# The router of a mixture-of-experts layer: order of its VectorE work, register loads, split gather and the start of the expert products

## What is computed

```python
aff = sigmoid(xt @ router_w)                       # 256 tokens, 16 experts in 4 groups of 4
biased = aff + router_bias
group_score = sum(top_k(biased grouped by 4, 2))   # best two of each group
g_sel = argmax(group_score)                        # one group for each token
e_idx = top_k(where(in_group, biased, -inf), 2)    # two experts inside it
gates = one_hot(e_idx) * aff / sum of the two
out = sum_e (silu(xt @ w_gate[e]) * (xt @ w_up[e]) * gates[e]) @ w_down[e]   # 1024 -> 512 -> 1024
```

## Time and profile before

| | |
|---|---|
| median of 3 runs | 3359.07 us (3356.76 to 3362.08) |
| the profiled execution | 3353.76 us, its span 3351.9 us |
| mean granted TensorE clock | 0.96 of full speed |
| busy | PE 92%, PEld 72%, DVE 49%, ACT 31% of the span |
| instructions | 40558 |
| HBM | 475.95 MB read, 142 GB/s over the span |

### The profile page before, as it was taken

The page is one execution under the profiler, slowest core; times in us unless marked ns, Lnnn a source line. Parts: engine busy times, 40 slices in busy tenths (PEclk is TensorE's granted clock), DMA queues, the critical chain, the costliest instruction groups (busy, mean ns, idle before and its releaser), DMA issues.

```text
span 3351.9 us, 40558 instructions
## 1 busy us (share of the span) xinstructions
PE 3070.9 (92%) x16552; PEld 2410.8 (72%) x16552; DVE 1642.7 (49%) x2593; ACT 1047.7 (31%) x1584; POOL 16.4 (0%) x56
## 2 busy tenths in 40 slices
PE   8779999988999799998997877899999999986998
PEld 7568876766887588884445777378886888855898
DVE  1545487245448643333975666263335324324554
ACT  2333376234337622222022111142224222132333
POOL 0000000000000000000000000000000000000000
PEclk9999999989999899999998888999999999998999
DMA  6437698544779722223122000322221222220452
GB/s 257 181 132 287 264 354 311 179 167 174 278 271 349 284 85 92 100 100 127 69 80 91 1 1 1 151 92 96 101 100 63 100 101 91 85 76 0 148 179 101
DMA packets 69102, 479.22 MB, mean 143 GB/s; under 512 B 7376, under 2 KB 10832, under 8 KB 11728
## 3 DMA queue, kind: packets, MB, share of 16 engines
q1 hardware_dynamic: 67616, 473.16, 37.8%
q10 hardware_dynamic: 1328, 3.87, 0.3%
HBM read 475.95 MB, written 1.05 MB: 142 GB/s over the span
## 4 chain that ended last, share of the span: by engine, by line
PE 68%; PEld 8%; DVE 8%; issue 6%; ACT 4%; PEldq 3%; DMA 2%; DVEq 0%; ACTq 0%; SPq 0%
PE ps L541 18%; PE ps L542 18%; PE ps L543 18%; PEld ps L533 8%; PE ps L533 2%; PE ps L1473 1%; PE ps L1764 1%; PE ps L2075 1%; DMA ring<-in_ada 1%; PE ps L1488 1%; PE ps L2087 1%; ACT w_hi L554 1%; PE ps L2346 1%; PE ps L808 1%; PE ps L1545 1%
## 5 line engine op out<-in xcount | busy, mean ns | idle before, releaser
L562 DVE TENSOR_TENSOR w_lo<-ring,w_hi 128x1024 fp32r<-128x1024 f32 x552 | 671.1, 1224 | 712.1 <-ACT w_hi L554 705.7
L554 ACT ACTIVATE w_hi<-ring 128x1024 fp32r<-128x1024 f32 x552 | 582.2, 1058 | 922.5 <-PE ps L543 767.3
L541 PE MATMUL ps<-x_hi,w_hi 128*128 128x512 f32 (+1 forms) x1408 | 514.8, 366 | 23.2 <-DVE x_lo L928 12.5
L542 PE MATMUL ps<-x_lo,w_hi 128*128 128x512 f32 (+1 forms) x1408 | 513.3, 365 | 0.0
L543 PE MATMUL ps<-x_hi,w_lo 128*128 128x512 f32 (+1 forms) x1408 | 513.2, 364 | 0.0
L541 PEld LDWEIGHTS ps<-x_hi,w_hi 128*128 128x128 f32 x1408 | 268.1, 190 | 68.9 <-issue 24.1
L533 PE MATMUL ps<-HM,ring 128*128 128x256 f32 (+1 forms) x928 | 296.6, 481 | 12.4 <-DVEq L963 3.7
L542 PEld LDWEIGHTS ps<-x_lo,w_hi 128*128 128x128 f32 x1408 | 268.1, 190 | 41.4
L543 PEld LDWEIGHTS ps<-x_hi,w_lo 128*128 128x128 f32 x1408 | 267.8, 190 | 41.7
L533 PEld LDWEIGHTS ps<-HM,ring 128*128 128x128 f32 x928 | 177.5, 192 | 129.1 <-issue 110.4
L541 PE MATMUL ps<-h_hi,w_hi 128*128 128x512 f32 (+1 forms) x704 | 255.2, 362 | 0.0
(11 more groups left out here) (407 smaller groups left out, 4448.8 us busy)
## 6 DMA issues: line engine op xcount, KB each, us to landing
ring<-in_moe_up SPq DMA_DIRECT2D x128, 1024.0 KB, 5.2
ring<-in_ff_up SPq DMA_DIRECT2D x88, 1024.0 KB, 4.7
ring<-in_ada SPq DMA_DIRECT2D x72, 1024.0 KB, 6.2
ring<-in_moe_down SPq DMA_DIRECT2D x64, 1024.0 KB, 5.2
ring<-in_ff_down SPq DMA_DIRECT2D x44, 1024.0 KB, 4.7
ring<-in_w_in SPq DMA_DIRECT2D x14, 1024.0 KB, 7.6
ring<-in_even_in SPq DMA_DIRECT2D x10, 1024.0 KB, 4.7
ring<-in_w_o SPq DMA_DIRECT2D x8, 1024.0 KB, 7.5
```

The lines of the kernel that those rows point to most:

```text
L541: pe.matmul(dst, hi, xh, start=start, stop=False, skip_group_check=True)
L542: pe.matmul(dst, hi, xl, start=False, stop=False, skip_group_check=True)
L554: act.activation(w_hi[:, j % HALVES, :], ring[:, u % SLOTS, (j % 2) * D:(j % 2 + 1) * D], ACT.Copy)\
L562: dve.tensor_tensor(w_lo[:, j % HALVES, :], ring[:, u % SLOTS, (j % 2) * D:(j % 2 + 1) * D], w_hi[:, j % HALVES, :].bitcast(F32), ALU.subt ...
```

## The change

- DVE: the eight m_lo move from the head of `router_dve` to behind S_; the routing starts at once. Behind them the low halves 0 and 1 of the first unit are made, ahead of the gates; halves 2 and 3 stay behind the gates.
- SP: only the first group id is read before the first expert transfer; the three others are read before the first unit of another rank, the fifth.
- Gather: the turned x is kept as a high part XT_hi (ACT's copy, now to fp32r) and a low part XT_lo (DVE, `turned_rest(0)` ahead of the wait for "counts", `turned_rest(1)` behind S_). S_ is now written as fp32r, S_r. The two products of each k become four, all with fp32r operands. Groups 6 and 7 go to banks 2 and 3 and wait for ACT's copies 2 and 3; all groups wait for `turned_rest(1)`.
- PE: `moe_pe` no longer waits for the end of the router on all engines, but for ACT's copy 1 and for m_lo; then, as before, for each split half. `gates()` waits for copy 7 and for step "gates".
- The new tiles lie in the memory that the split operands of the other stages use; XG, ST_ and the rest keep theirs by a placeholder.

```diff
--- before.py
+++ after.py
@@ -72,6 +72,7 @@
 SLOT_N = sum(RANK_SLOTS)
 SIDE_ROWS = (P, 88, P)
 SIDE_N = sum(SIDE_ROWS)
+ROUTING = DC * SLOT_N + 3 * PER_GROUP + 3 * T + SIDE_N + 4 * 64 + 32 * E_N + TT * E_N + 16 * 16
 FF_SEGS = (12, 10)
 MOD_UNITS = N_MOD * D // 256
 MOD_GROUP = 4
@@ -195,7 +196,12 @@
                 m_hi, m_lo = part(other, "m_hi", [P, DC, T]), part(other, "m_lo", [P, DC, T])
                 e_hi, e_lo = part(other, "e_hi", [P, HALVES, T]), part(other, "e_lo", [P, HALVES, T])
                 gate_b = part(other, "gate_b", [P, PER_GROUP, T], F32)
+                with ExitStack() as early:
+                    XT_lo = part(early, "XT_lo", [P, TT, D])
                 xg_hi, xg_lo = part(other, "xg_hi", [P, DC, SPLIT_SLOTS]), part(other, "xg_lo", [P, DC, SPLIT_SLOTS])
+                S_r = part(other, "S_r", [P, TT, SIDE_N])
+                part(other, "routing", [P, ROUTING])
+                XT_hi = part(other, "XT_hi", [P, TT, D])
         HM = sb("HM", [P, DC, N2])
         AREA = 24000
         area = sb("area", [P, AREA])
@@ -260,11 +266,12 @@
         SQ = Space(4096).take(DC, N2)
         VM = Space(12288).take(DC, N2)
 
-        s = Space(11264 + 2 * DC * SPLIT_SLOTS)
+        s = Space(11264 + 2 * DC * SPLIT_SLOTS + TT * SIDE_N)
+        S_ = S_r[:].bitcast(F32)
         XG, GS = s.take(DC, SLOT_N), s.take(len(RANK_SLOTS), PER_GROUP)
-        S_, ST_, SLOTS_ = s.take(TT, SIDE_N), s.take(len(RANK_SLOTS), T), s.take(SIDE_N)
+        ST_, SLOTS_ = s.take(len(RANK_SLOTS), T), s.take(SIDE_N)
         HT3, R, G, M4 = s.take(2, 2, 64), s.take(16, 2 * E_N), s.take(TT, E_N), s.take(16, 16)
-        XT_ = Space(s.at).take(TT, D)
+        assert s.at == 11264 + 2 * DC * SPLIT_SLOTS + TT * SIDE_N + ROUTING
         YR = s.take(len(RANK_SLOTS), D)
         GB = s.take(TT * PER_GROUP, P)
 
@@ -363,6 +370,7 @@
                 MOE_UNITS += [("A", 1 + p_ // PAIRS, p_ % PAIRS), ("B", 1 + p_ // PAIRS, p_ % PAIRS)]
             if p_ >= 2:
                 MOE_UNITS.append(("D", 1 + (p_ - 2) // PAIRS, (p_ - 2) % PAIRS))
+        FIRST_UNITS = next(i for i, u in enumerate(MOE_UNITS) if u[1])
         HALF_AT = {u: 2 * i for i, u in enumerate(u for u in MOE_UNITS if u[1] < 3)}
         HALF_N = 2 * len(HALF_AT)
 
@@ -444,7 +452,7 @@
             modulation_site(n + "ln1", 4, (4, 5))
             st = stage(n + "router", pe=["logits", "turn0", "turn1", "counts", "sides", *[f"got{k}" for k in range(DC)]],
                        act=["exp", "turn0", "turn1", "sides", *[f"got{k}" for k in range(DC)]],
-                       dve=["groups", "order", "select", "gates4", "gates"])
+                       dve=["groups", "rest0", "order", "select", "rest1", "gates4", "gates"])
             st.x0 = count["x"]
             count["x"] += DC
             moe_stage(n + "moe", l)
@@ -516,7 +524,9 @@
                     enter(sp, n)
                     sp.dma_start(SLOTS_, w["slots"]).then_inc(slots_in, 16)
                     sp.wait_ge(dve_done, stages[n].v("dve", "order"))
-                    picked = [sp.value_load(group_ids[0:1, k:k + 1], min_val=0, max_val=GROUPS - 1) for k in range(GROUPS)]
+                    picked = [sp.value_load(group_ids[0:1, 0:1], min_val=0, max_val=GROUPS - 1)]
+                if u - FIRST_UNITS in order_at:
+                    picked += [sp.value_load(group_ids[0:1, k:k + 1], min_val=0, max_val=GROUPS - 1) for k in range(1, GROUPS)]
                 if u >= SLOTS:
                     sp.wait_ge(*streams[u - SLOTS][2:])
                 sp.dma_start(ring[:, u % SLOTS, 0:width], source(picked)).then_inc(arrived[u % SLOTS], 16)
@@ -1278,6 +1288,10 @@
             return (out_.rearrange("p b (e d) -> p b e d", e=2),
                     inverse.rearrange("p (e b) -> p b e", e=2).unsqueeze(3).broadcast_to([P, 4, 2, VD]))
 
+        def got_bank(k):
+
+            return k if k < 6 else k - 4
+
         def router_pe(pe, n):
             st = enter(pe, n)
             pe.wait_ge(act_done, st.v("act", "exp"))
@@ -1301,10 +1315,11 @@
                     ins = pe.transpose(ps[0:m, 7 - r // 2, (r + 1) % 2 * T + t * P:(r + 1) % 2 * T + (t + 1) * P], S_[:, t, a:a + m], ident)
             ins.then_inc(pe_done, st.one("pe", "sides"))
             pe.wait_ge(act_done, st.v("act", "turn1"))
+            pe.wait_ge(dve_done, st.v("dve", "rest1"))
             for k in range(DC):
-                if k == 6:
-                    pe.wait_ge(act_done, st.v("act", "sides"))
-                dot(pe, ps[:, k, 0:SLOT_N], [(XT_[:, t, k * P:(k + 1) * P], S_[:, t, 0:SLOT_N]) for t in range(TT)])\
+                if k >= 6:
+                    pe.wait_ge(act_done, st.v("act", f"got{k - 4}"))
+                dot(pe, ps[:, got_bank(k), 0:SLOT_N], [(x_[:, t, k * P:(k + 1) * P], S_r[:, t, 0:SLOT_N]) for x_ in (XT_hi, XT_lo) for t in range(TT)])\
                     .then_inc(pe_done, st.one("pe", f"got{k}"))
             pe.drain().then_inc(pe_done, 1)
 
@@ -1315,7 +1330,7 @@
                 act.activation(m_hi[:, k, :], X[:, k, 0:T], ACT.Copy).then_inc(xhi_done, 1)
             for t in range(TT):
                 act.wait_ge(pe_done, st.v("pe", f"turn{t}"))
-                act.activation(XT_[:, t, :].rearrange("p (a b) -> p a b", a=2), ps[:, 2 + 2 * t:4 + 2 * t, :], ACT.Copy)\
+                act.activation(XT_hi[:, t, :].rearrange("p (a b) -> p a b", a=2), ps[:, 2 + 2 * t:4 + 2 * t, :], ACT.Copy)\
                    .then_inc(act_done, st.one("act", f"turn{t}"))
             act.wait_ge(pe_done, st.v("pe", "sides"))
             for r, m in enumerate(SIDE_ROWS):
@@ -1324,7 +1339,7 @@
             tables_silu(act)
             for k in range(DC):
                 act.wait_ge(pe_done, st.v("pe", f"got{k}"))
-                act.activation(XG[:, k, :], ps[:, k, 0:SLOT_N], ACT.Copy).then_inc(act_done, st.one("act", f"got{k}"))
+                act.activation(XG[:, k, :], ps[:, got_bank(k), 0:SLOT_N], ACT.Copy).then_inc(act_done, st.one("act", f"got{k}"))
                 if k % 2:
                     split_hi(act, stages[follows], k // 2, None)
             act.drain().then_inc(act_done, 1)
@@ -1332,9 +1347,13 @@
         def router_dve(dve, link, n, l, follows):
 
             st = enter(dve, n)
-            for k in range(DC):
-                dve.wait_ge(xhi_done, st.x0 + k + 1)
-                dve.tensor_tensor(m_lo[:, k, :], X[:, k, 0:T], m_hi[:, k, :].bitcast(F32), ALU.subtract).then_inc(xlo_done, 1)
+
+            def turned_rest(t):
+                dve.wait_ge(act_done, st.v("act", f"turn{t}"))
+                dve.tensor_tensor(XT_lo[:, t, :].rearrange("p (a b) -> p a b", a=2), ps[:, 2 + 2 * t:4 + 2 * t, :],
+                                  XT_hi[:, t, :].rearrange("p (a b) -> p a b", a=2).bitcast(F32), ALU.subtract)\
+                    .then_inc(dve_done, st.one("dve", f"rest{t}"))
+
             dve.wait_ge(pe_done, st.v("pe", "logits"))
             flat = lambda i: R[:, i, :]
             te = lambda i: R[:, i, :].rearrange("p (t e) -> p t e", t=TT)
@@ -1371,6 +1390,7 @@
             link(dve.tensor_tensor(ge(2), ge(2), inner(ing, 4), ALU.mult))
             dve.wait_ge(dve_done, st.v("dve", "groups"))
             link(dve.tensor_tensor(ge(2), ge(2), inner(R[:, 5, 0:8], 4), ALU.add))
+            turned_rest(0)
 
 
             sq = lambda i: M4[:, i, :].rearrange("p (a b) -> p a b", a=4)
@@ -1395,8 +1415,13 @@
             link(dve.tensor_reduce(slot, two(5), AXX, ALU.add))
             dve.wait_ge(slots_in, 16 * (l + 1))
             for t in range(TT):
-                ins = dve.tensor_scalar(S_[:, t, :], SLOTS_, slot[:, t:t + 1], None, ALU.is_equal)
+                ins = dve.tensor_scalar(S_r[:, t, :], SLOTS_, slot[:, t:t + 1], None, ALU.is_equal)
             ins.then_inc(dve_done, st.one("dve", "select"))
+            turned_rest(1)
+            for k in range(DC):
+                dve.wait_ge(xhi_done, st.x0 + k + 1)
+                dve.tensor_tensor(m_lo[:, k, :], X[:, k, 0:T], m_hi[:, k, :].bitcast(F32), ALU.subtract).then_inc(xlo_done, 1)
+            split_first(dve, split_lo, follows, 0, 2)
 
             first_best(te(2), con("first16"), te(6), E_N)
             link(dve.scalar_tensor_tensor(flat(2), flat(6), NEG, flat(2), ALU.mult, ALU.add))
@@ -1412,7 +1437,7 @@
             dve.wait_ge(dve_done, st.v("dve", "gates4"))
             link(dve.tensor_tensor(two(8), two(7), inner(inbig, PER_GROUP), ALU.mult))
             dve.tensor_copy(GB, inner(M4[:, 8, 0:8], P)).then_inc(dve_done, st.one("dve", "gates"))
-            split_first(dve, split_lo, follows)
+            split_first(dve, split_lo, follows, 2)
             dve.drain().then_inc(dve_done, 1)
 
 
@@ -1421,7 +1446,9 @@
             return ps[:, 4 + d // 2, d % 2 * T:(d % 2 + 1) * T]
 
         def moe_pe(pe, n):
-            st = enter(pe, n)
+            st, routed = stages[n], stages[n[:-3] + "router"]
+            pe.wait_ge(act_done, routed.v("act", "got1"))
+            pe.wait_ge(xlo_done, routed.x0 + DC)
 
```

(2 more changed lines are left out.)

## The result

The changed kernel takes 3330.85 us (3329.67 to 3335.51, 4 runs) against 3360.57 for the kernel before in the same comparison: ratio 0.9914, 95% interval 0.9897 to 0.9932. Timed a second time it had ratio 0.9933 (0.9916 to 0.9951), some 22 us. The profiled executions, 3353.76 and 3331.63 us, lie 22.1 us apart.

A forecast was written before the change was run, and what follows sets the result against it. TensorE with its weight loads, three quarters of the span, was taken as the bound. Earlier ends of `up_big(0)` in both layers summed to 17.8 us (18.65 at full clock, 17.0 at low): 3359.07 - 17.8 = 3341.3 us, range 3335 to 3350.

The forecast's parts named there:

- Rival C: Behind the routers: only the lead of the transfers counts, 9.3 us gained, 3349.8 us; chance 0.10.
- D: Gather: fp32r products of 280 columns cost as much as fp32 ones, 0.7 us slower in all; chance 0.03.
- B: First expert product: halves 0 and 1 run at 1.2 GHz in both layers, gain 12.6 us, 3346.5; chance 0.20.
- A2: First expert transfer lands after 4.9 us, sum 21.0, 3338 us; chance 0.62 together with the main forecast.
- The routing: Start of the router on DVE: with m_lo moved away, it begins 2.65 us earlier in each layer.
- the loads: SP ahead of the first expert transfer: three fewer group id loads, 1.65 us earlier in each layer.
- the landing: First expert transfer of each layer: lands 6.75 us after its issue, at 214.2 and 788.3 us.
- Step 3: First expert transfer: one group id read saves 1.65 us, issue at 207.5 us in layer 0, landing 6.75 us later.
- Layer 1's bound of 4.9: First expert transfer in layer 1: rows showed 4.9 us or less to land; kept only for the range.
- the clock of half 0: First half of `up_big(0)`: 1.2 GHz in one layer of two, 17.8 us between 18.65 and 17.0.
- Low half 2: DVE behind the gates: ready at 224.0 and 798.05 us, with PE waiting 1 to 2 us for it.
- the median: Whole kernel: the same 17.8 us gain carried over to the median, which lies 5.3 us above the profiled execution.

The follow-up runs named there:

- ids4: The changed kernel with all four group ids read ahead of the first expert transfer; 3340.70 us, ratio 0.9949 to the kernel before.
- b_pe_order: The kernel before with TensorE's early start and low halves 0 and 1 ahead of the gates' chain; 3349.58 us, ratio 0.9975.
- gather_only: The kernel before with only the gather in single-pass products of the turned x's high and low parts; 3357.02 us, ratio 0.9991.
- b_route: The kernel before with only the eight m_lo moved behind the selection; 3351.36 us, ratio 0.9981.
- b_pe: The kernel before with only TensorE's early start, waiting for copy 1, m_lo and a split half; 3347.31 us, ratio 0.9970.
- mlo_first: The changed kernel with the eight m_lo ahead of the routing again; 3344.58 us, ratio 0.9960 to the kernel before.

## Why the prediction was wrong

**Which way, and where: right.** The stage, the absence of any loss behind it and the mechanism held. The mixture of experts took the lead over whole: from the end of `up_big(0)` of layer 0 to the last send-back of its ranks the positions agree within 0.11 us before and after on PE. Rival C is out, D too (the gather ran as single passes, in 6.6 us with the low clock over most of it). B did not happen: `up_big(0)` ran at 2.4 GHz. What came is A2, the earlier landing, with half 0 at full clock.

**The routing, the loads: right.** Issue forecast 4.25 and 5.05 us earlier, measured 4.31 and 5.09. `turned_rest(0)` at 1.25, measured 1.22.

**The first wrong term: the landing.** Step 3 took "6.75, the same four transfers" for both layers and kept 4.9 for the range. It was 4.8 us in both. The first high half came 1.7 and 1.5 us before its forecast position (13.16 and 13.17 behind the slots' transfer, forecast 14.9 and 14.7), and with it low halves, gates and half 2. That is 3.3 us, near the 3.2 that A2 gave it. It was not worth more because ACT, with its copies and the table load, was ready only 0.24 us behind the landing. The reason given for 6.75, that four transfers share the engines, does not hold: the same four stood behind each other at 4.8. Layer 1's bound of 4.9 stood in the rows, and it was the better guide of the two. (The Trainium skill, DMA: Bandwidth & Descriptors, Anatomy of one DMA, gave 4.4 us as an estimate; the landing measured here is 0.4 us above that, so it was nearer than the row that the sum used.)

**The second: the clock of half 0.** The sum charged 1.2 GHz to half 0 in one layer of two, 0.85 us. The low stretch fell on sides and gather instead. (The Trainium skill's warning, TensorE: Matmul & The Clock Gate, HAM oscillation — how this bites in real kernels, agrees with the sides and the gather behind them, at a granted clock of 0.50 behind a pause of 3.33 us; the products of half 0 had no such pause ahead of them, 0.26 us.) With both terms put right the sum is 17.8 + 3.3 + 0.85 = 21.95 us, and the profiled routers give 22.0. Low half 2 is on the path as forecast; PE waits about 0.2 us for it in layer 0 and 0.50 in layer 1, where 1 to 2 were forecast.

**The third: the median.** The sum was carried over as if the changed kernel's median, too, would lie 5.3 us above its profiled execution; it lay 0.8 below in the first comparison, 3 above in the second. The repeated kernels show single runs over 20 us (3347.10 to 3367.13) for the kernel before. The first comparison's 29.7 us between the medians and the second's 24.8 are two draws around a gain whose part in the routers is 22.0; the intervals of the two overlap from 0.9916 to 0.9932, which is 23 to 28 us. What lies above 22 I can't assign to an edit. The spread of one kernel's runs goes with the granted clock: in the 84 runs of the kernel before that were timed beside the experiments, the median was 3350.2 us at a mean granted clock of 0.962, 3352.9 at 0.961, 3358.5 at 0.959 and 3363.5 at 0.957. The changed kernel's four runs of the first comparison had 0.961 to 0.963. In which stage a run that is not profiled gains or loses clock is not shown. Between profiles of different kernels the scan at about 1720 to 2180 us is the place that moves by several us; the two profiles of one kernel, though, agree behind the second router to 0.1 us, so that it moves from one execution to the next is argued and not shown. So a step failed here, too: the lower edge of the range, 3335, allowed 2 to 3 us for the medians, and should have allowed the spread of both. With the routers' 22.0 us alone the median would have been 3337, inside it.

**How the parts share the gain.** They do not add. Alone on the kernel before, early start, routing, one id and gather give 12.9, 9.4, 2.1 and 1.1 us, 25.5 in all; together, with the order of the low halves, 22.0. Taken away one at a time from the changed kernel they cost 17.9, 7.0, 4.5 and 6.0, and the order 3.0. So gather and one id are worth little on the old order, where something else is awaited (the 2.1 of one id is clock alone), and 4 to 6 us on the new one; the early start grows from 12.9 to 17.9 as the halves come sooner, by starts of half 0 from 9.1 to 15.7. Parts of each figure are the clock, as said with each run, and with one profile of each kernel they are good to about a microsecond a layer.

## What to carry to other kernels

Where an engine waits at a stage's border for everything of the stage before, look first at what it needs for its first instruction: that wait alone was worth more than any other edit here, and it made the others worth something. Order on a queue has no value of its own: the same two splits ahead of the same chain gained 1.3 us a layer where the queue was busy until their data came; where it was not, they brought PE a wait of 1.00 us in one layer and gained nothing in the other. Before a difference between two kernels is put down to an edit, look at whether the stretch that it changed is the one that differs: in two of the runs here it was the clock of another. And when one profile has two layers with the same transfer at 6.75 and at 4.9 us, a forecast should carry both as equal cases.

## What the runs showed of the hardware

The first 1 MB expert transfer of a layer took one of two times. In layer 0 it landed in 6.1 to 6.7 us in five of the seven profiles with four group ids read ahead of it (the kernel before twice, ids4, b_pe_order, gather_only), in 4.8 to 4.9 in the two others (b_route, b_pe) and in 4.7 to 4.8 in all nine profiles with one id. In layer 1 it was 4.7 to 4.9 everywhere. The moment of the issue behind the slots' transfer does not decide it: mlo_first issued at 11.62 us and had 4.8, ids4 at 9.80 and had 6.2. Both kernels that were profiled twice showed the same value twice, to 0.1 us.

The traces hold a candidate for the cause. In layer 0 every profile has one packet of 16 KB of the kind "instruction" on DMA queue 8 near this transfer. For the kernel before, from issue to landing (211.73 to 218.4 us), the view of the DMA queues has it, and for the changed kernel (208.96 to 213.76) it has not:

```profile
q1 hardware_dynamic: 234, 1.79, 79.4%
q8 instruction: 1, 0.02, 0.9%
```

```profile
q1 hardware_dynamic: 185, 1.38, 77.0%
```

Counted from the issue, this packet starts at 0.08 to 3.07 us in the five profiles with the slow landing, and at 4.6 to 5.9 us, when the transfer is done or nearly so, in the nine with one id. In layer 1 no profile has it before 11 us, and every landing there is short. Of the two fast ones with four ids, b_route has it from 0.04 to 0.98 us, ahead of the transfer's first data packet at 1.00; b_pe has it from 0.20 to 1.49 and lands in 4.9 all the same, which such a collision alone does not explain. Where the packet starts within 0.6 us of the issue (five profiles), SP also issues its third transfer late, 1.5 to 2.1 us behind the first; in the eleven others it is 1.1. So the register loads may act by where they put this packet, and not by their own time. No run moves the packet alone, and the cause stays open.

The clock took part in most differences. Moving work by its own length often moved the end by more: mlo_first lost 3.5 us a layer by a move of 2.65, and b_route gained 9.4 in both where the earlier start gave 7.1, each time because a stretch at 1.2 GHz moved onto or off work that was waited for.
